# Sliding attention with the values two halves behind the scores, and the first head's scores ahead of its projections

## The chip, the cores and the metric

One core of one Trainium2 chip. The metric is the device time of one execution in microseconds, as a median of the runs. Operands and results are float32; matrix products are made of three products of rounded high parts and low remainders.

## What is computed

The program runs two blocks on 512 tokens of width 1024: a differential attention layer and a sliding-window attention layer with feed-forward parts, then a convolution mixer and a windowed attention with a context of 256 tokens, again with feed-forward parts. The change touches the first two attentions. The first, cut to what matters (8 heads, two score maps of 64 features each per head):

```python
s = jnp.einsum('bqhcd,bkhcd->bhcqk', qblk, k).astype(jnp.float32) * scale
p = jax.nn.softmax(jnp.where(causal, s, NEG_INF), axis=-1)
a = p[:, :, 0] - lam * p[:, :, 1]
return jnp.einsum('bhqk,bkhe->bqhe', a.astype(v.dtype), v)
```

The sliding one (4 key heads, 4 query heads to each, window 128, so a tile of 128 queries sees its own tile of keys and the one before):

```python
s = jnp.einsum('bnqhgd,bnkhd->bnhgqk', qb, kw).astype(jnp.float32) * (1.0 / math.sqrt(HEAD_DIM))
s = jnp.where(valid[None, :, None, None], s, NEG_INF)
m = jnp.maximum(jnp.max(s, axis=-1, keepdims=True), sink)
e = jnp.exp(s - m)
p = e / (jnp.sum(e, axis=-1, keepdims=True) + jnp.exp(sink - m))
o = jnp.einsum('bnhgqk,bnkhd->bnqhgd', p.astype(vw.dtype), vw)
```

## The kernel before

Each engine has an order written out by hand; semaphores join them. Nothing is planned at run time, and each engine takes its instructions in that order. The stages follow each other: `heads` (first attention), its output projection, feed-forward, `kv` and `q` (sliding attention), its output projection, and so on.

**First attention.** A slot is one tile of 128 queries of one head; a head has four slots, and tile i sees i + 1 tiles of keys. TensorE's `slot` (line 2143) makes the scores, transposes the previous slot's weights (`turn`), projects queries, keys and values of one tile of the next head (`project`, line 2082), multiplies the previous slot's values (`values`), and transposes one tile of queries and keys (`turn_qk`). ScalarE's `slot` (983) makes the exponentials (988), copies the transposed weights (960), rounds the weights of the head after next (980), evacuates the projection (940 to 947) and copies turned queries and keys (952). VectorE's `slot` (1678) makes maxima (1683), norm and rotation (`rope`, 1626 to 1632), combines the two maps (1641 to 1646) and makes the low parts of the weights (1673). In the first head the tiles of head 1 were projected one before and one just after the first `turn_qk`, and two in slots 2 and 3.

**Sliding attention.** `swa` runs over 16 groups m of four query heads and one tile (key head m // 4, tile m % 4), each in two halves p = 2m and 2m + 1 of two heads. Names by engine:
- TensorE: `scores(p)` (2303), one masking product of bf16 and four of f32; `turn(p, 0)` (2342) transposes the exponentials; `turn_q(m)` (2295) transposes the queries; `project(m, k0, k1)` (2270) steps k0 to k1 of eight, three matmuls each; `values(p, 0)` (2356); `spread_inverse(m)` (2369); `begun` starts the output projection early.
- ScalarE: `evac_proj(m)` (1087, 1089), `turned(m)` (1095), `exps(p, x)` (1105, x the head in the half), `weights(p, c)` (1117) copies transposed exponentials, `sinks(m)` (1123), `spread_out(m)` (1130) copies the spread inverses out of PSUM, `outs(m)` (1136) the high part of the outputs, `refill` (1148) and `split` (763) high parts of weights.
- VectorE: `maxima(p)` (1836, 1840, 1843), `rotated(m)` (1601 to 1614), `doubled(m)` (1809), `q_low(m)` (1814), `sink_args(m)` (1851), `inverses(m)` (1860, 1862), `outputs(m)` (1867), `low_outs(m)` (1874), `refill` (1311) and `split` (1303) low parts.
- GpSimd: the roots of `rotated` (564) and the widening of the inverses (698).

`outputs(m)` waits for `spread_out(m)`, that for `spread_inverse(m)`, that for the inverses. Scores use three places in PSUM by turns, the transposes two banks by turns in an order that `turn_order` (418) lists: a transpose waits until the one two before it has been read. The context variant of the same function (with 256 context keys) is used by the last attention.

In the loop before, weights of half p are transposed, copied and multiplied in half p + 1, and queries of group m + 2 are turned in the odd half of group m.

Of the kernel before, what the change touches and what calls it, by code (L numbers as in the profile page):

```python
# [178 lines left out]
def program(nc, dram, out):  # L179
    stages = make_plan()  # L180
    stack = ExitStack()
    with stack:
# [25 lines left out]
        half = sbuf("half", [P, 24])  # L208
# [209 lines left out]
        def turn_order(st):  # L418

            order = [("q", 0), ("q", 1)]  # L420
            for p in range(33):
# [286 lines left out]
        def _(act):  # L708
# [222 lines left out]
            def heads(st):  # L931
                S = s_da
# [50 lines left out]
                def slot(h, par, i, first=False, more=True, new=True):  # L983
# [7 lines left out]
                    if not (first and i == 0):  # L991
                        weights(j - 1, (i - 1) % 4)
# [19 lines left out]
                for t in range(3):  # L1012
                    turned(t, t, 0)
# [65 lines left out]
            def swa(st):  # L1079
# [75 lines left out]

                evac_proj(0)
# [5 lines left out]
                for p in range(34):  # L1162
                    m, half = p // 2, p % 2
                    parts = len(chunks(st, p - 1)) if 0 < p < 33 else 0
                    if half == 0 and m < 14:
                        evac_proj(m + 2)
                    if half and m:
                        spread_out(m - 1)
                    if parts:
                        weights(p - 1, 0)  # L1170
                    if p < 32:
                        exps(p, 0)
                    if parts > 1:
                        weights(p - 1, 1)
                    if p < 32:
                        exps(p, 1)
                    if parts > 2:
                        weights(p - 1, 2)
                    if half and m < 16:
                        sinks(m)  # L1180
                    if half and m < 14:
                        turned(m + 2)
                    if half and m:
                        outs(m - 1)
                    if m in (2, 3, 6, 7):
                        refill(m // 4 + 2, p % 4)
                    if p in OUT_SPLITS:
                        split(st["after"], OUT_SPLITS.index(p), OUT_SPLITS.index(p))
# [20 lines left out]
        def _(dve):  # L1209
# [578 lines left out]
            def swa(st):  # L1788
# [112 lines left out]
                for p in range(35):  # L1901
                    m, half = p // 2, p % 2
                    if half == 0 and 0 < m < 17:
                        inverses(m - 1)
                    if half == 0 and m >= 2:
                        low_outs(m - 2)
                    if p < 32:
                        maxima(p)
                    if half and m:
                        outputs(m - 1)  # L1910
                    if half == 0 and 0 < m < 15 and not st["ctx"]:
                        q_low(m + 1)
                    if half == 0 and m < 14:
                        rotated(m + 2)
                        doubled(m + 2)
                    if half and m < 16:
# [28 lines left out]
        def _(pe):  # L1945
# [133 lines left out]
            def heads(st):  # L2079
# [63 lines left out]
                def slot(h, par, i, first=False, more=True):  # L2143
# [11 lines left out]
                    if more and not (first and i < 2):  # L2155
                        project(j + 4, i, 1 - par, h + 1)
# [109 lines left out]
            def swa(st):  # L2266
# [108 lines left out]

                pe.wait_ge(S["kpe"], nt + 1)
# [8 lines left out]
                for p in range(33):  # L2385
                    m, half = p // 2, p % 2
                    parts = len(chunks(st, p - 1)) if p else 0
                    k0 = 4 * half
                    if p < 32:
                        scores(p)  # L2390
                    if parts:
                        turn(p - 1, 0)
# [136 lines left out]
```

## Time and profile before

| | us |
|---|---|
| runs: median (lowest to highest of 3) | 2894.04 (2886.19 to 2899.03) |
| the profiled execution | 2895.21 |
| its span | 2893.2 |
| TensorE busy in it | 2778.1 (96%) |
| VectorE, ScalarE, GpSimd busy | 1777.6, 1115.5, 161.3 |

The profiled execution's own time is the span and 2.0 us around it. The page gives the busy time of each engine, then the span in 40 slices, DMA queues, the chain that ended last, and the costliest groups of instructions. TensorE's busy time counts a modelled end of each matmul, so a start-to-start distance says more about it than a duration. The first head of the first attention lies at 40 to 77 us, the sliding loop at 744 to 905 us.

### The profile page before, as it was taken

The numbers are of one execution on the slowest core, as the hardware profiler recorded it, in microseconds if no ns is written. First come the engines' busy times: TensorE is split into PE (matmuls) and PEld (weight loads), VectorE is DVE, ScalarE is ACT, GpSimd is POOL, SyncE is SP. The second block draws the span as 40 slices with busy tenths as digits, with TensorE's granted clock in tenths as the row PEclk, the third lists the DMA queues.
The fourth block names the chain that finished last, engine by engine and source line by source line (L and its number), as shares of the span: only waits on it lengthen the run. The fifth ranks groups of instructions, "written<-read, shape, count | busy, mean of one in ns | idle before, by whom it ended". The sixth has DMA issues, their size and how long they took to land.

```text
span 2893.2 us, 41339 instructions
## 1 busy us (share of the span) xinstructions
PE 2778.1 (96%) x14371; PEld 2314.3 (80%) x14371; DVE 1777.6 (61%) x2765; ACT 1115.5 (39%) x1869; POOL 161.3 (6%) x205
## 2 busy tenths in 40 slices
PE   7999999999788999999998999999999999999998
PEld 6887788888777778887886888888888887788886
DVE  6775667675765676767885654453456655564645
ACT  5554322224664322223433332231224666442432
POOL 4121000001110000000210000000000000000000
PEclk8999999999999999999998999999999999999999
DMA  3211345452011344542651112112111000222221
GB/s 130 65 45 59 124 164 185 167 182 81 30 37 52 141 172 167 182 148 71 147 139 44 51 59 70 62 58 67 60 57 45 16 30 30 69 99 92 98 89 65
DMA packets 75218, 263.72 MB, mean 91 GB/s; under 512 B 8496, under 2 KB 10800, under 8 KB 73264
## 3 DMA queue, kind: packets, MB, share of 16 engines
q1 hardware_dynamic: 70880, 249.99, 25.1%
q0 software_dynamic: 4176, 11.63, 2.2%
q8 instruction: 94, 1.54, 0.2%
q14 instruction: 68, 0.56, 0.1%
HBM read 247.87 MB, written 2.10 MB: 86 GB/s over the span
## 4 chain that ended last, share of the span: by engine, by line
PE 62%; issue 15%; DVE 13%; ACT 6%; DVEq 2%; ACTq 1%; DMA 1%; POOLq 1%; POOL 0%; SPq 0%
PE psum L1948 16%; PE psum L1950 16%; PE psum L1949 16%; DVE w_lo L1303 2%; PE psum L2113 2%; DVE work L1473 2%; ACT work L1105 2%; PE psum L2091 1%; PE psum L2092 1%; PE psum L2093 1%; PE psum L2365 1%; ACT w_hi L763 1%; ACT sw_pt L1117 1%; DVE work L1591 1%; ACT work L814 1%
## 5 line engine op out<-in xcount | busy, mean ns | idle before, releaser
L1948 PE MATMUL psum<-hx_hi,w_hi 128*128 128x512 f32 x1568 | 622.9, 397 | 4.7 <-DVE hc_lo L1582 1.7
L1950 PE MATMUL psum<-hx_hi,w_lo 128*128 128x512 f32 x1568 | 620.6, 396 | 0.0
L1949 PE MATMUL psum<-hx_lo,w_hi 128*128 128x512 f32 x1568 | 620.0, 395 | 0.0
L763 ACT ACTIVATE w_hi<-w_raw 128x1024 fp32r<-128x1024 f32 (+1 forms) x328 | 344.8, 1051 | 512.8 <-PE psum L1950 207.5
L1303 DVE TENSOR_TENSOR w_lo<-w_raw,w_hi 128x1024 fp32r<-128x1024 f32 (+1 forms) x328 | 398.2, 1214 | 201.1 <-ACT w_hi L763 183.5
L1950 PEld LDWEIGHTS psum<-hx_hi,w_lo 128*128 128x128 f32 x1568 | 295.0, 188 | 70.0
L1948 PEld LDWEIGHTS psum<-hx_hi,w_hi 128*128 128x128 f32 x1568 | 295.0, 188 | 63.7 <-issue 5.4
L1949 PEld LDWEIGHTS psum<-hx_lo,w_hi 128*128 128x128 f32 x1568 | 295.1, 188 | 47.5
L1948 PE MATMUL psum<-a_hi,w_hi 128*128 128x512 f32 (+1 forms) x656 | 233.3, 356 | 9.9 <-DVE a_lo L1413 8.9
L1949 PE MATMUL psum<-a_lo,w_hi 128*128 128x512 f32 (+1 forms) x656 | 232.8, 355 | 0.0
L1950 PE MATMUL psum<-a_hi,w_lo 128*128 128x512 f32 (+1 forms) x656 | 232.6, 355 | 0.0
L1948 PE MATMUL psum<-o_hi,w_hi 128*128 128x512 f32 x544 | 219.7, 404 | 2.7 <-DVE w_lo L1303 2.7
L1949 PE MATMUL psum<-o_lo,w_hi 128*128 128x512 f32 x544 | 217.2, 399 | 0.0
L1950 PE MATMUL psum<-o_hi,w_lo 128*128 128x512 f32 x544 | 217.1, 399 | 0.0
L1435 DVE SCALAR_TENSOR_TENSOR work<-psum,vec,work 128x511 f32<-128x511 f32 (+1 forms) x132 | 83.2, 658 | 162.7 <-ACT work L844 154.4
L564 POOL TENSOR_TENSOR tok_r<-tok_ms,half 128x4 f32<-128x4 f32 (+1 forms) x62 | 67.2, 1084 | 1891.0 <-DVE tok_ms L1231 1577.0
L1377 DVE SCALAR_TENSOR_TENSOR X<-psum,mods,X 128x512 f32<-128x512 f32 x96 | 60.6, 659 | 172.1 <-PE psum L1950 169.8
L844 ACT ACTIVATE work<-psum,vec 128x768 f32<-128x768 f32 (+1 forms) x88 | 70.1, 796 | 220.8 <-PE psum L1950 212.3
L1948 PEld LDWEIGHTS psum<-a_hi,w_hi 128*128 128x128 f32 x656 | 124.3, 190 | 29.4 <-DVE a_lo L1413 9.5
L1948 PE MATMUL psum<-hc_hi,w_hi 128*128 128x256 f32 x512 | 144.6, 282 | 0.0
L1949 PE MATMUL psum<-hc_lo,w_hi 128*128 128x256 f32 x512 | 143.9, 281 | 0.0
L1950 PE MATMUL psum<-hc_hi,w_lo 128*128 128x256 f32 x512 | 143.3, 280 | 0.0
(310 smaller groups left out, 4918.5 us busy)
## 6 DMA issues: line engine op xcount, KB each, us to landing
mod_w<-in_w_mod SPq DMA_DIRECT2D x96, 512.0 KB, 3.7
w_raw<-in_fup SPq DMA_DIRECT2D x88, 512.0 KB, 4.6
w_raw<-in_cup SPq DMA_DIRECT2D x88, 512.0 KB, 3.6
w_raw<-in_fdown SPq DMA_DIRECT2D x32, 512.0 KB, 4.6
w_raw<-in_cdown SPq DMA_DIRECT2D x32, 512.0 KB, 3.6
sw_vb<-tap_prod POOLq DMA_DIRECT2D x29, 391.5 KB, 5.1
w_raw<-in_da_qkv SPq DMA_DIRECT2D x18, 512.0 KB, 3.6
w_raw<-in_fdown SPq DMA_DIRECT2D x16, 384.0 KB, 3.3
```

The lines of the kernel that those rows point to most:

```text
L564: pool.tensor_tensor(tok_r[:, a:b], tok_ms[:, a:b], half[:, a:b], ALU.pow).then_inc(done, 1)
L763: r = act.activation(w_hi[:, off:off + n], w_raw[:, raw:raw + n], ACT.Copy)
L844: act.activation(wk[:, s, 0:toks], ps_of(st, s, 0, toks), ACT.Copy, scale=vec[:, bass.ds(b + col, 1)]).then_inc(s_ctap, 1)
L1105: r = act.activation(work[:, e:e + (w1 - w0)], psum[:, w0:w1], ACT.Exp, bias=neg_max[:, col:col + 1], scale=root, accum_out=row_sum[:, col ...
L1303: r = dve.tensor_tensor(w_lo[:, off:off + n], w_raw[:, raw:raw + n], w_hi[:, off:off + n].bitcast(F32), ALU.subtract)
L1377: r = dve.scalar_tensor_tensor(X[:, b, a:e], ps_of(st, s, a, e), mods[:, l, c, bass.ds(b + o, 1)], X[:, b, a:e], ALU.mult, ALU.add)
L1435: dve.scalar_tensor_tensor(dst[:, a + 1:e], src(a, e - 1), prev, dst[:, a + 1:e], ALU.mult, ALU.add)
L1473: dve.scalar_tensor_tensor(acc, u[:, j:j + n], w, acc, ALU.mult, ALU.add)
L1948: pe.matmul(dst, wh, xh, start=first, stop=False)
L1949: pe.matmul(dst, wh, xl, start=False, stop=False)
L1950: return pe.matmul(dst, wl, xh, start=False, stop=last)
L2113: r = pe.matmul(pb[:, 2 + c, 0:n], qT[rows_, i * P:(i + 1) * P], qT[rows_, SEQ:SEQ + n], start=True, stop=False)
```

## The change

In the first head, `project` for tiles 1 to 3 of head 1 moves to slots 0 to 2, behind the scores, and the second and third `turn_qk` with ScalarE's copies move into slot 0 behind them.

In the sliding attention (not in the variant with context, which keeps its order in functions of its own) the orders of all three engines are new. On TensorE weights of half p are transposed at the end of half p + 1 and multiplied in half p + 2; queries of group m + 1 are turned in the even half of group m, right behind the scores; four projection steps stand in the even half, two and two in the odd; `spread_inverse(m - 1)` moves to the odd half. ScalarE copies the weights of half p - 2 first, and copies turned queries and spread inverses in the even half behind the exponentials. VectorE takes the maxima first in each half, makes the outputs in the even half and low queries, rotation and doubling in the odd one. The loops are one half longer on TensorE and VectorE, two on ScalarE.

```diff
         def turn_order(st):
 
             order = [("q", 0), ("q", 1)]
+            if not st["ctx"]:
+                for p in range(33):
+                    if p % 2 == 0 and 1 <= p // 2 <= 14:
+                        order.append(("q", p // 2 + 1))
+                    if p:
+                        order.append(("e", chunk0(st, p - 1)))
+                return order
             for p in range(33):
...
@@ -988,7 +995,10 @@
                         act.activation(work[:, 1024 * (i % 2) + 512 * c:1024 * (i % 2) + 512 * c + (i + 1) * P],
                                        pb[:, 2 + c, 0:(i + 1) * P], ACT.Exp, bias=neg_max[:, u:u + 1],
                                        accum_out=row_sum[:, u:u + 1]).then_inc(S["ex"], 1)
-                    if not (first and i == 0):
+                    if first and i == 0:
+                        turned(1, 1, 0)
+                        turned(2, 2, 0)
+                    else:
                         weights(j - 1, (i - 1) % 4)
                     if i == 1 and not first:
...
-                for t in range(3):
-                    turned(t, t, 0)
+                turned(0, 0, 0)
                 for i in range(4):
                     slot(0, 0, i, first=True)
...
+                def loop_late(st):
+                    for p in range(36):
+                        m, half = p // 2, p % 2
+                        if 2 <= p < 34:
+                            weights(p - 2, 0)
+                        if half == 0 and m < 14:
+                            evac_proj(m + 2)
+                        if p < 32:
+                            exps(p, 0)
+                            exps(p, 1)
+                        if half == 0 and 1 <= m <= 14:
+                            turned(m + 1)
+                        if half == 0 and m >= 2:
+                            spread_out(m - 2)
+                        if half and m < 16:
+                            sinks(m)
+                        if half and m >= 2:
+                            outs(m - 2)
+                        if m in (2, 3, 6, 7):
+                            refill(m // 4 + 2, p % 4)
+                        if p in OUT_SPLITS:
+                            split(st["after"], OUT_SPLITS.index(p), OUT_SPLITS.index(p))
+
...
-                for p in range(35):
+                for p in range(35 if st["ctx"] else 36):
                     m, half = p // 2, p % 2
-                    if half == 0 and 0 < m < 17:
-                        inverses(m - 1)
-                    if half == 0 and m >= 2:
-                        low_outs(m - 2)
-                    if p < 32:
-                        maxima(p)
-                    if half and m:
-                        outputs(m - 1)
-                    if half == 0 and 0 < m < 15 and not st["ctx"]:
-                        q_low(m + 1)
-                    if half == 0 and m < 14:
-                        rotated(m + 2)
-                        doubled(m + 2)
-                    if half and m < 16:
-                        sink_args(m)
-                    if half and m < 14 and st["ctx"]:
-                        q_low(m + 2)
+                    if st["ctx"]:
+                        if half == 0 and 0 < m < 17:
+                            inverses(m - 1)
+                        if half == 0 and m >= 2:
+                            low_outs(m - 2)
+                        if p < 32:
+                            maxima(p)
+                        if half and m:
+                            outputs(m - 1)
+                        if half == 0 and m < 14:
+                            rotated(m + 2)
+                            doubled(m + 2)
+                        if half and m < 16:
+                            sink_args(m)
+                        if half and m < 14:
+                            q_low(m + 2)
+                    else:
+                        if p < 32:
+                            maxima(p)
+                        if half == 0 and 0 < m < 17:
+                            inverses(m - 1)
+                        if half == 0 and m >= 2:
+                            outputs(m - 2)
+                        if half and m < 16:
+                            sink_args(m)
+                        if half and 1 <= m <= 14:
+                            q_low(m + 1)
+                        if half and m < 14:
+                            rotated(m + 2)
+                            doubled(m + 2)
+                        if half and m >= 2:
+                            low_outs(m - 2)
...
@@ -2152,7 +2205,12 @@
                     if i == 3 and not first:
                         pe.wait_ge(S["qte"], j + 3 if more else 32)
                         turn_outputs(h - 1)
-                    if more and not (first and i < 2):
+                    if first and i < 3:
+                        project(i + 5, i + 1, 1, 1)
+                    if first and i == 0:
+                        turn_qk(1, 1)
+                        turn_qk(2, 2)
+                    if more and not first:
                         project(j + 4, i, 1 - par, h + 1)
                     if not (first and i == 0):
                         if i == 1 and not first:
@@ -2186,10 +2244,6 @@
                 project(4, 0, 1, 1)
                 pe.wait_ge(s_in, 16 * LOADS_IN)
                 turn_qk(0, 0)
-                pe.wait_ge(S["pje"], 2)
-                project(5, 1, 1, 1)
-                turn_qk(1, 1)
-                turn_qk(2, 2)
                 pe.wait_ge(S["pje"], 4)
                 pe.wait_ge(s_constb, 1)
                 for i in range(4):
...
+                def early_output(p):
+                    if p == 27:
+                        pe.wait_ge(S["pje"], 16)
+                    begun(st["after"], 0, (0, 1, 2, 4, 5)[p - 27], (1, 2, 4, 5, 6)[p - 27])
+
+                def loop_late():
+                    for p in range(34):
+                        m, half = p // 2, p % 2
+                        if p < 32:
+                            scores(p)
+                        if half == 0 and 1 <= m <= 14:
+                            turn_q(m + 1)
+                        if half and m < 13:
+                            project(m + 3, 4, 6)
+                        if p >= 2:
+                            values(p - 2, 0)
+                        if half == 0 and m < 13:
+                            project(m + 3, 0, 4)
+                        if half and m < 13:
+                            project(m + 3, 6, 8)
+                        if 27 <= p < 32:
+                            early_output(p)
+                        if 0 < p < 33:
+                            turn(p - 1, 0)
+                        if p == 32:
+                            pe.wait_ge(S["ex"], 30)
+                            begun(st["after"], 3, 0, 6)
+                        if half and m:
+                            spread_inverse(m - 1)
```

`loop_ctx` on each engine is the old loop, called where there is a context; `loop_late` takes its place where there is none. VectorE's loop body is the old one under the condition of a context.

## Rows read from the trace of the kernel before

**Rows 1.** Windows: from:to, length, busy us (xinstructions) by engine; TensorE clock, DMA share, GB/s.

```profile
...
76.00:109.00 33.00, 33.00 (x189) 28.37 (x189) 24.48 (x55) 19.68 (x56) 6.95 (x7) 1.00 0.22 65
745.60:898.80 153.20, 121.92 (x776) 108.35 (x776) 102.77 (x277) 100.54 (x258) 20.32 (x29) 0.92 0.09 32
830.00:832.00 2.00, 2.00 (x8) 1.64 (x7) 1.65 (x5) 0.88 (x4) 1.01 (x1) 0.50 0.02 4
...
```

**Rows 2.** Timeline, first head: start us, us, engine, line, operation, count, [idle before <-releaser].

```profile
...
40.60 0.39 ACT L952 ACTIVATE da_T<-psum 128x256 f32<-128x256 f32 x1 [2.32 <-PE psum L2101]
...
49.89 0.48 PE L2101 MATMUL psum<-ident,da_qk 128*128 128x128 f32 x1 [2.74 <-DVE da_qk L1632]
...
76.91 0.42 PE L2091 MATMUL psum<-w_hi,hx_hi 128*128 128x384 f32 x1
...
```

**Rows 3.** Timeline, same columns: slot 3 of the first head, slot 1 of head 1.

```profile
...
67.60 1.12 PE L2113 MATMUL psum<-da_T 64*128 64x512 f32 x2
...
74.65 1.23 DVE L1673 TENSOR_TENSOR w_lo<-w_raw,w_hi 128x1024 fp32r<-128x1024 f32 x1
...
82.43 0.70 PE L2113 MATMUL psum<-da_T 64*128 64x256 f32 x2
...
83.95 0.42 PE L2091 MATMUL psum<-w_hi,hx_hi 128*128 128x384 f32 x1
```

**Rows 4.** Chain of waits, one sliding group: start us, us, engine, tile written, line.

```profile
...
842.77 0.69 DVE neg_max L1836
...
843.97 0.56 ACT work L1105
...
844.69 0.56 ACT work L1105
...
845.72 0.60 ACT sw_qa L1095
...
846.39 0.43 ACT o_hi L1136
846.85 0.43 DVE o_lo L1874
...
847.36 0.69 DVE neg_max L1836
...
848.62 0.69 DVE sw_qb L1814
...
851.29 0.69 DVE sw_dup L1809
...
852.07 0.69 DVE neg_max L1836
...
```

**Rows 5.** Timeline, columns as in rows 2: sliding steps that the chain lacks.

```profile
...
840.98 0.39 ACT L1130 ACTIVATE sw_invb<-psum 128x256 f32<-128x256 f32 x1 [0.34 <-PE psum L2372]
...
824.73 0.16 DVE L1851 TENSOR_TENSOR sink_e<-neg_max,neg_sink 128x4 f32<-128x4 f32 x1
824.99 0.88 DVE L1311 SCALAR_TENSOR_TENSOR w_lo<-w_raw,vec,w_hi 128x256 fp32r<-128x256 f32 x2
...
```

**Rows 6.** Timeline, TensorE, in the sliding loop.

```profile
...
829.02 0.39 PE L2281 MATMUL psum<-w_hi,hx_hi 128*128 128x256 f32 x1 [1.95 <-ACT sw_sq L1089]
...
```

**Rows 7.** Timeline, start and end of the sliding loop.

```profile
...
748.96 0.42 DVE L1836 TENSOR_REDUCE neg_max<-psum 128x2 f32<-128x256 f32 x1
...
767.45 0.69 DVE L1836 TENSOR_REDUCE neg_max<-psum 128x2 f32<-128x512 f32 x1
...
896.38 0.69 DVE L1836 TENSOR_REDUCE neg_max<-psum 128x2 f32<-128x512 f32 x1
...
904.14 0.69 PE L2353 MATMUL psum<-ident,work 128*128 128x128 f32 x4 [1.55 <-ACT work L1105]
...
```

**Rows 8.** Page, costliest groups: line, operation, count | busy us, mean ns | idle before, releaser.

```profile
...
L763 ACT ACTIVATE w_hi<-w_raw 128x1024 fp32r<-128x1024 f32 (+1 forms) x328 | 344.8, 1051 | 512.8 <-PE psum L1950 207.5
L1303 DVE TENSOR_TENSOR w_lo<-w_raw,w_hi 128x1024 fp32r<-128x1024 f32 (+1 forms) x328 | 398.2, 1214 | 201.1 <-ACT w_hi L763 183.5
...
```

More of the change, by code:

```diff
@@ L1161, in swa @@
                 turned(1)
-                for p in range(34):
-                    m, half = p // 2, p % 2
-                    parts = len(chunks(st, p - 1)) if 0 < p < 33 else 0
-                    if half == 0 and m < 14:
-                        evac_proj(m + 2)
-                    if half and m:
-                        spread_out(m - 1)
-                    if parts:
-                        weights(p - 1, 0)
-                    if p < 32:
[L1172 to L1178, printed above, removed]
-                    if half and m < 16:
[L1180 to L1188, printed above, removed]
+                if st["ctx"]:
+                    loop_ctx(st)
+                else:
+                    loop_late(st)
             for st in stages:
@@ new lines, in loop_ctx @@
+                def loop_ctx():
+                    for p in range(33):
+                        m, half = p // 2, p % 2
+                        parts = len(chunks(st, p - 1)) if p else 0
+                        k0 = 4 * half
+                        if p < 32:
+                            scores(p)
+                        if parts:
+                            turn(p - 1, 0)
+                        if parts > 1:
+                            turn(p - 1, 1)
+                        if half and m < 14:
+                            turn_q(m + 2)
+                        if m < 13:
+                            project(m + 3, k0, k0 + 2)
+                        elif 27 <= p < 32:
+                            early_output(p)
+                        elif p == 32:
+                            pe.wait_ge(S["ex"], 64)
+                            begun(st["after"], 3, 0, 6)
+                        if parts:
+                            values(p - 1, 0)
+                        if parts > 2:
+                            turn(p - 1, 2)
+                        if m < 13:
+                            project(m + 3, k0 + 2, k0 + 4)
+                        for c in range(1, parts):
+                            values(p - 1, c)
+                        if half == 0 and m:
+                            spread_inverse(m - 1)
@@ L2384, in swa @@
                 turn_q(1)
[L2385 to L2392, printed above, removed]
[L2393 to L2416 removed]
+                if st["ctx"]:
+                    loop_ctx()
+                else:
+                    loop_late()
                 wo = st["after"]
```

58 lines of the change are left out of this document (30 added, 28 removed).

## The prediction

> **What bounds the kernel now.** I read the page first (TensorE busy 96% of the span), then the windows, to find the stretches where that is not so, then the timeline and the chain of waits inside them. In head 1 of the first attention TensorE is busy for all 33 us of a 33 us stretch at full clock, so in that stage time saved ahead of it stays saved. In the sliding loop it is busy 121.9 of 153.2 us at a mean clock of 0.92, VectorE 102.8, ScalarE 100.5 [rows 1]: none of the three is full. The reader should look there for what passes the work around.
>
> The chain of waits of one full-width group of two halves shows it [rows 4]. VectorE takes the maxima (842.77), ScalarE does two exponentials (843.97, 844.69), the sinks, the copy of the turned queries (845.72) and the high half of the outputs (846.39), VectorE the low half (846.85), the next maxima (847.36), the queries' low half (848.62), rotation and doubling (851.29), and is back at maxima at 852.07: 9.30 us. TensorE is not in it. Where it does enter, it is through a late evacuation of the projection: a gap of 1.95 us, and TensorE is at 0.50 of its clock right after [rows 1, 6].
>
> In the first head TensorE has nothing to project in its first two slots: one wait alone is 2.74 us (49.89), and head 1's first projection begins at 76.91 [rows 2].
>
> **The change part by part.**
>
> *First head.* The three projections for head 1 move from before slot 0 and slots 2, 3 to slots 0, 1, 2. No instruction is added. The anchor is ScalarE's copy of the first turned queries, which ends at 40.60 + 0.39 = 40.99 [rows 2]; the scores now start there. Costs of the pieces: scores of two tiles plus a turn 83.95 - 82.43 = 1.52; three tiles 0.42 more (1.12 - 0.70 over one head is 0.42 for two tiles more, so 0.21 per tile and head), one tile 0.42 less. Projection, eight value products and two transposes run from 76.91 to 82.43, 5.52; without most of the value products I estimate a projection at 4.3 [rows 2, 3].
> - Slot 0: 41.0 + 1.1 + 4.3 = 46.4, then three pairs of transposes with a ScalarE copy (0.39) between each, about 2.3: 48.7.
> - Slot 1: 1.5 + 4.3 + 0.5 = 6.3: 55.0. Slot 2: 1.9 + 0.1 + 4.3 + 0.7 = 7.0: 62.0.
> - Slot 3 has no projection left, so it is bound by ScalarE and VectorE. In the trace VectorE's low weights for head 2 end 74.65 + 1.23 - 67.60 = 8.28 after the scores of slot 3 begin [rows 3], and head 1's first projection waits for them: 62.0 + 8.3 = 70.3, against 76.91. That is 6.5 us sooner.
>
> What is next late: in slot 3 TensorE now idles about 3 us in three pieces. If the clock falls there, the projection behind it starts at half rate and gives some 1.5 us back, for good, because TensorE is full from then on. Bounds -6.5 and -2 us; I take **-5.5**.
>
> *Sliding attention, the new wait.* Values trail by two halves, and the output steps move. On VectorE an even half is now maxima, inverses, **outputs**; but outputs need the spread inverses, which ScalarE copies only after both exponentials and the turned queries of that same half, and those need these maxima. Before, that copy came first in a half on ScalarE. VectorE is in order, so queued behind the waiting outputs are the odd half's maxima, sink arguments, low queries, rotation and doubling; TensorE's next turn of the queries waits for the doubling, ScalarE's exponentials for the maxima. The new ring, each step by its row:
> - even half: maxima to exponentials 1.20 (843.97 - 842.77), two exponentials 2 x 0.72, turned queries 0.67 (846.39 - 845.72), spread copy 0.39 + 0.05, outputs 0.51 (as 846.85 to 847.36, the same 256 columns): 4.26 [rows 4, 5];
> - odd half: maxima 1.25 (848.62 - 847.36), sink arguments 0.26 (824.99 - 824.73), low queries and rotation 2.67, doubling 0.78, low outputs 0.51: 5.47 [rows 4, 5].
>
> Sum 9.73 against 9.30: the ring gets **longer** by 0.43 us a group. It swaps the sinks (845.72 - 844.69 - 0.72 = 0.31) and the high outputs (0.46) for the spread copy, outputs and sink arguments (0.44 + 0.51 + 0.26). A group whose tile is the first has half the columns; its two reductions are 0.42 rather than 0.69, so 9.19 [rows 4, 7].
>
> *Sliding attention, the waits removed.* TensorE no longer turns the exponentials, has them copied and multiplies them within one half. In steady groups that hides nothing, since TensorE was not in the ring. It pays at the start and around refills. Start: the first maxima at 748.96 do not move. Then two narrow maxima (0.98 each), sink arguments, rotation and doubling (2.67 less the low queries' 0.69 + 0.1, and 0.78: 2.66) give the second group's maxima at 753.8; TensorE's 29 matmuls between doubling and the second half's scores, at the loop's mean of 121.92/776 = 0.157 us, take 4.6 us, to 758.3; 4.96 more (1.25 + 0.26 + 2.67 + 0.78) puts the third group's maxima at 763.3, where the trace has 767.45: 4.1 us sooner [rows 1, 4, 7].
>
> From there to group 14: nine full and three narrow groups, 9 x 9.73 + 3 x 9.19 = 115.1. Eight refill steps on VectorE, 0.88 + 0.1 each, 7.8 [rows 5]; ScalarE's part of them is now beside other work. Two splits of the output weights sit in even halves: ScalarE's 1.05 starts only after the spread copy (3.75), VectorE's 1.21 after that, so the half ends at 6.21 rather than 4.26, twice 1.95 [rows 8]. Group 14: 126.8 after 763.3, that is 890.1. It has no rotation but one split: 9.73 - 2.66 + 1.95 = 9.02, so the last group's maxima are at 899.1 (before 896.38). Its even half has a split and no turned queries: 1.20 + 1.44 + 0.44 + 1.15 + 1.31 = 5.54, to 904.7, and the exponentials end 1.20 + 1.44 later at 907.3 [rows 4, 7].
>
> *The tail.* In the last halves TensorE must multiply half 30 before it turns half 31, but ScalarE copies half 30's weights only after half 31's exponentials, sinks (0.31) and high outputs (0.46), and the copy takes 0.7 (as the turned queries, 512 columns): 908.8; four products at 0.157 make it 909.4. Before, the last turn was at 904.14 [rows 7]. Behind it TensorE has the same full run of output-projection work in both. Loop: 909.4 - 904.14, **+5.3 us**. Ends: -1, if the copies before the turns run further ahead than counted, and +12, by the first rival below.
>
> The sum is -5.5 + 5.3, about 0. The profiled execution took 2895.21 us (span 2893.2), 1.2 above the median of the runs, 2894.04; by it the changed kernel profiles at 2895, and in the median I say **2894.5**.
>
> **The rivals.**
>
> *TensorE becomes late in the odd half.* Between the doubling and the odd half's scores stand 29 matmuls. At 0.157 each that is 4.6 us from 0.6 before the even maxima: ready at 4.0, needed at 4.26. At half clock (8 matmuls in the 2 us from 830, 0.25 each) they take up to 7.2, ready at 6.6, at most 2.3 us late; I take 1.5, since such a stretch need not cover all of them [rows 1, 6]. It decides from the point where the gap ahead of the turned queries reaches about 1.9 us, as the one that went before the 0.50 stretch. For it: VectorE's queue holds TensorE back in every group. Against: the turn of the even half's weights now waits for a bank that the low queries free, which cuts the idle time into about 0.7 and 1.1 us. If half of the 14 groups fall to half clock, + 7 x 1.5 = 10 us (2905); if nearly all, + 20 (2915). The Trainium skill, "TensorE: Matmul & The Clock Gate", section on HAM oscillation, warns only of idle gaps longer than any in this loop; by it this rival would be worth nothing, while the row at 830 shows 0.50 behind a 1.95 us gap, and I go by the row. Chance **0.14**, and this is the slower side.
>
> *The decoupling works as it says.* If the spread copy finds ScalarE free ahead of the exponentials, so that outputs do not wait, VectorE's own work is the ring: 9.73 less the wait of 3.75 - 1.75 = 2.0, near 7.8 us a group, 24 us over the loop less what TensorE then holds back (its 121.9 busy us leave room for it): 2868 to 2880. For it: every TensorE wait of the loop does get another half of time. Against: the order on ScalarE is written out, and the exponentials stand ahead of that copy. Chance **0.08**.
>
> *The first head gives nothing.* Slot 3's waits drop the clock and the low weights for head 2 come no earlier against TensorE: gain 1 us rather than 5.5, 2899. Against: the idle time of slots 0 and 1 is plain in the trace and is filled. Chance **0.14**.
>
> The forecast has **0.64**, with a range of its own from 2887 to 2902.
>
> **How the numbers follow.** The range takes in the first-head rival and the milder half of the late-TensorE one, and below it a loop that costs nothing (-5.3) plus the spread of the runs shown (2886 to 2899): 2883 to 2906. Half a per cent is 14.5 us, about what can be told from no change. Faster by more needs the decoupling rival: 0.08. Slower by more than 2908.5 needs TensorE late in most groups: 0.08. The same: 0.84.
>
> **What would show it.** In the chain of waits of the loop, the ring from one even half's maxima to the next should be 9.6 to 9.9 us, with the outputs idle about 2 us before them, released by the spread copy on ScalarE. The third group's maxima should come near 763 less the first head's gain, all later times shifted alike; the last turn of weights some 5 us later than before relative to the first maxima. Head 1's first projection should start near 70 to 71. The forecast is wrong if outputs do not wait, if a wait of maxima on TensorE's scores is in most groups, or if the clock over the loop is under 0.88.

## The result, and the profile after

The changed kernel takes 2903.65 us (median of 17 runs, 2898.89 to 2911.3) against 2894.51 us for the kernel before (17 runs beside them): ratio 1.0027, 95% interval 1.002 to 1.0034. That is 9.1 us slower, within half a per cent. It is inside the range of 2883 to 2906, 2.35 us under its upper end, and just outside the range of 2887 to 2902 that the forecast itself had. The profiled execution of the changed kernel took 2906.14 us. Its page begins so (busy us, share, xinstructions):

```profile
span 2904.1 us, 41339 instructions
...
PE 2781.3 (96%) x14371; PEld 2316.1 (80%) x14371; DVE 1777.9 (61%) x2765; ACT 1114.7 (38%) x1869; POOL 160.3 (6%) x205
```

TensorE is as full as before by its share; the loss has to be looked for in the stages where it is not.

The sliding loop does what the chain was summed up to do. Chain of waits of one group (start us, us, engine, tile written, line), the answer to [rows 4]:

```profile
845.24 0.69 DVE neg_max L1874
...
847.90 0.60 ACT sw_qa L1104
...
848.63 0.39 ACT sw_invb L1139
849.05 0.42 DVE sw_osb L1905
...
849.56 0.69 DVE neg_max L1874
...
853.74 0.69 DVE sw_dup L1847
...
854.53 0.42 DVE o_lo L1912
...
855.04 0.69 DVE neg_max L1874
```

From maxima to maxima it is 9.80 us, where it was 9.30. The spread copy (`sw_invb`) stands behind the exponentials and the turned queries, and VectorE's outputs (`sw_osb`) behind it. What engines waited for in 735 to 910 us (waiting line <- releaser: us in total, times, longest us):

```profile
DVE sw_osb L1905 <- ACT sw_invb L1139: 26.8, 14, 2.0
...
PE psum L2419 <- ACT sw_pt L1126: 22.2, 14, 3.0
...
PE psum L2353 <- DVE sw_dup L1847: 16.1, 15, 1.5
...
DVE neg_max L1874 <- PE psum L2392: 4.0, 2, 2.3
```

VectorE waits for the copy fourteen times, once a group, up to 2.0 us each, and the odd half's work is queued behind these waits. The maxima wait for TensorE only twice, so TensorE does not set the groups. Windows of the changed kernel (columns as in [rows 1]): 33 us from head 1's first projection; the sliding loop from first to last group's maxima; and the end of that loop.

```profile
71.78:104.78 33.00, 33.00 (x184) 28.55 (x183) 24.22 (x55) 19.57 (x55) 6.94 (x7) 0.98 0.22 65
746.77:900.13 153.36, 113.10 (x731) 100.30 (x730) 97.38 (x262) 96.39 (x249) 19.66 (x28) 0.94 0.09 32
...
892.00:899.00 7.00, 5.53 (x16) 4.48 (x17) 3.52 (x7) 3.22 (x9) 0.00 (x0) 0.53 0.23 75
```

The clock over the loop is 0.94 (before 0.92), so it is not half rate that makes the loop long, except at its end. Timeline of the changed kernel there and in the first head (columns as in [rows 2]):

```profile
67.31 1.65 PE L2186 MATMUL psum<-da_v,da_aT 128*128 128x128 f32 x6 [1.64 <-ACT da_aT L967]
...
71.78 0.67 PE L2144 MATMUL psum<-w_hi,hx_hi 128*128 128x384 f32 x1
...
887.72 0.69 DVE L1874 TENSOR_REDUCE neg_max<-psum 128x2 f32<-128x512 f32 x1
...
893.47 2.07 PE L2419 MATMUL psum<-sw_pt,sw_vb 128*128 128x256 f32 x4 [2.96 <-ACT sw_pt L1126]
...
900.13 0.69 DVE L1874 TENSOR_REDUCE neg_max<-psum 128x2 f32<-128x512 f32 x1 [2.27 <-PE psum L2392]
```

Head 1's first projection starts at 71.78 instead of 76.91 [rows 2], 5.1 us sooner, but it takes 0.67 us instead of 0.42, at half rate behind slot 3's waits.

Stage by stage, in us. The stages are cut at the first operation of each norm (VectorE's reading of `tok_ms` from PSUM). Each entry is the mean, the lowest and highest, and the number of the profiled executions with the order named; for the sliding stage these are the versions with the order of before or of the change, without the variants further down:

```
stage                      old order             new order             difference
heads (first attention)    289.7 (287.4-290.6) 5   287.6 (283.8-288.6) 9   -2.1
sliding attention          239.7 (237.5-241.8) 5   249.0 (246.7-250.8) 4   +9.3
network behind the convolution     567.2 or 574.0          567.2 or 574.0           see below
first profile of each kernel: heads -3.0, sliding +7.4, network behind the convolution +6.8,
all else -0.3; sum +10.9, the 10.9 us between the two profiled executions
```

### The profile page after: what moved, and what is told of

The parts are those of the page before. It is cut to its first block, busy times and chain, and to the rows that moved or that the text cites. A ratio compares the mean times of both kernels' runs of the same rounds, so it can differ in the third digit from the quotient of the medians.

```text
span 2904.1 us, 41339 instructions
## 1 busy us (share of the span) xinstructions
PE 2781.3 (96%) x14371; PEld 2316.1 (80%) x14371; DVE 1777.9 (61%) x2765; ACT 1114.7 (38%) x1869; POOL 160.3 (6%) x205
## 4 chain that ended last, share of the span: by engine, by line
PE 64%; issue 15%; DVE 12%; ACT 6%; DVEq 2%; POOLq 1%; ACTq 0%; POOL 0%
PE psum L2001 17%; PE psum L2002 17%; PE psum L2003 17%; DVE w_lo L1341 2%; PE psum L2166 2%; ACT work L1114 2%; DVE work L1511 1%; PE psum L2144 1%; PE psum L2145 1%; PE psum L2146 1%; PE psum L2419 1%; ACT w_hi L770 1%; ACT sw_pt L1126 1%; DVE work L1629 1%; ACT work L821 1%
```

## Experiments: the two parts apart

The theory is that the first head gains and that the sliding order loses by the wait it puts on VectorE. The rival is something else in either part.

**head_only.** The kernel before with the first head's new order; what is projected and turned there, and nothing else of the diff.

```diff
+                    if first and i < 3:
+                        project(i + 5, i + 1, 1, 1)
...
-                for t in range(3):
-                    turned(t, t, 0)
+                turned(0, 0, 0)
```

> The changed order of the first head alone, in the kernel before; the sliding attention keeps its old order. Theory one (the first head gains what the trace of after shows, 4 to 5 us, and a clock drop at that stage's end takes part of it back): ratio to before 0.998 to 0.9995, head 1's first projection near 71 us rather than 76.9. Rival (the convolution feed-forward loops, 8.37 us a block before and 8.48 after, run slower because of how the new program is laid out): if that hangs on the first head's new order, the blocks here take 8.48 and the ratio is 1.000 to 1.001. Second rival (the block's length is drawn anew in each execution): it can be either here, whatever the order.

Measured: 2895.51 us, ratio 0.9997 (0.9988 to 1.0006). Its heads stage is 287.5 us, 3.1 under the 290.6 of the first profile of before, and 2.2 under the mean of the old order; the median can't be told from no change. Its network behind the convolution took 574.0 us, which the text had as the rival's sign; that is taken up further down.

**slide_only.** The changed kernel with the old first head.

> The new order of the sliding attention alone; the first head as before. Theory one (VectorE waits about 2 us in every group for the copy of the spread inverses, and the last halves wait for half 30's weights): slower by 6 to 8 us, ratio 1.002 to 1.003, ring of 9.8 us, fourteen waits of outputs on that copy of 1.7 to 2.0 us each. Rival (TensorE and its clock are what is late): the wait of the maxima on TensorE's scores is over 8 us in sum. Third (most of the measured 9 us lies in unchanged loops): ratio under 1.0015.

Measured: 2906.04 us beside 2896.0, ratio 1.0033 (1.002 to 1.0046). Heads 290.5, sliding 249.8. The fourteen waits of up to 2.0 us are there (26.9 us in all), and the maxima wait for TensorE once, 3.2 us, where the rival had over 8. The 10.0 us are over the 6 to 8 expected; the interval, 5.8 to 13.3 us, takes them in. The two parts, -0.5 and +10.0, add up to 9.5 where the whole change measured 9.1: no sign that they interact.

## Experiments: the wait on VectorE

**spread_first.** The changed kernel; in an even half ScalarE does the spread copy first.

```diff
                         if 2 <= p < 34:
+                            if half == 0 and m >= 2:
+                                spread_out(m - 2)
                             weights(p - 2, 0)
...
-                        if half == 0 and m >= 2:
-                            spread_out(m - 2)
```

> The changed kernel with one step moved: in each even half ScalarE copies the spread inverses first, ahead of the weights and the exponentials, not behind the turned queries. Theory one (that place is the cause of the slower ring): VectorE's 2 us wait ahead of the outputs goes; the ring falls from 9.8 us towards VectorE's own 7.8, but the products of TensorE (7.3 us a group plus waits for banks) may hold it at 8.2 to 9; over 14 groups 11 to 22 us less than the changed kernel, so 2882 to 2893, ratio to before 0.996 to 0.9995. Rival (TensorE's late scores bound the ring): it stays above 9.5 us, the wait of outputs turns into one of maxima on the scores, and the time stays within 3 us of the changed kernel's 2903.

Measured: 2886.51 us, ratio 0.9966 (0.9951 to 0.9981) to before; the sliding stage 232.7 instead of 248.9 us, 16.2 less, and the full-width groups without refill or split take 7.85 to 9.04 us. Timeline, VectorE in an even half:

```profile
833.81 0.69 DVE L1874 TENSOR_REDUCE neg_max<-psum 128x2 f32<-128x512 f32 x1
...
835.67 0.42 DVE L1905 TENSOR_TENSOR sw_osb<-psum,sw_invb 128x256 f32<-128x256 f32 x1
837.37 0.69 DVE L1874 TENSOR_REDUCE neg_max<-psum 128x2 f32<-128x512 f32 x1 [1.28 <-PE psum L2392]
...
842.85 0.69 DVE L1874 TENSOR_REDUCE neg_max<-psum 128x2 f32<-128x512 f32 x1
```

The outputs start without a wait, and the next wait is 1.28 us for TensorE's scores. This group takes 9.04 us (842.85 - 833.81) where the changed kernel took 9.80: part of the 2.0 us comes back as a wait for TensorE. TensorE's clock rises too, from a mean of 0.94 over the loop to 0.99, and how much of the 16.2 us is by that was not taken apart. Moving one copy turned a loss of 9 us into a gain of 9.5.

**outputs_late.** The same wait taken away from the other side: ScalarE as in the changed kernel, VectorE's outputs moved from the even to the odd half, behind its maxima.

> The changed kernel with VectorE's step outputs moved from the even half (behind the inverses) to the odd half (behind its maxima), so that ScalarE keeps its order, spread_out behind the exponentials and the turned queries. Theory (the new wait of 2.0 us on VectorE sets the length of a group, because the odd half's maxima are queued behind it): the wait vanishes as well as with spread_out moved first, the group goes from 9.8 to 8.3 to 8.8 us, the sliding stage from 248.9 to 233 us (231 to 236) and the time to 2888 us (2884 to 2892). Rival (what helped there was ScalarE's order itself, the weights or exponentials coming at another place): no gain, 2903 to 2907 us, and a group of 9.8 us.

Measured: 2895.18 us, ratio 0.9995 (0.9983 to 1.0007); the sliding stage 239.65 us. Of the 16.2 us of spread_first 9.2 come back, so neither text was right. Timeline, VectorE:

```profile
841.59 0.69 DVE L1874 TENSOR_REDUCE neg_max<-psum 128x2 f32<-128x512 f32 x1 [1.80 <-PE psum L2392]
...
842.84 0.42 DVE L1905 TENSOR_TENSOR sw_osb<-psum,sw_invb 128x256 f32<-128x256 f32 x1
...
847.58 0.69 DVE L1874 TENSOR_REDUCE neg_max<-psum 128x2 f32<-128x512 f32 x1
```

The wait for the copy is gone in this group (three are left in the loop and behind it, 5.2 us in all, one of 4.2 that spread_first has too). But the step's own time now lies in the odd half, where VectorE has no gap: 847.58 - 841.59 = 5.99 us, where spread_first has 842.85 - 837.37 = 5.48. In the even half the step was covered by the wait for scores, which is 1.80 here and 1.28 there. Group by group the loss against spread_first is 0.5 us in six groups, 0 to 0.4 in six, and 0.9 to 1.0 in the three from the first split of the output weights on (from the maxima at 847.58 in this version); 7.0 in all, the missing part. The step's own 0.51 us explains about half of the last three; what else is in them was not tested. VectorE's waits for ScalarE's high halves at the splits grew from 7.9 to 12.0 us, and TensorE's clock in these three groups was 0.96, 0.89 and 0.80 where spread_first had 1.00. So a wait can be removed from either engine, and the two are not worth the same: it counts in which half the step then stands.

**before_spread_last.** The wait put into the old order: the kernel before, with the spread copy of the odd half behind both exponentials.

```diff
-                    if half and m:
+                    if half and m and st["ctx"]:
                         spread_out(m - 1)
...
                     if p < 32:
                         exps(p, 1)
+                    if half and m and not st["ctx"]:
+                        spread_out(m - 1)
```

> The kernel before with one step moved: in the sliding stage's odd half ScalarE does spread_out behind both exponentials instead of first. The same wait is so put into the old order. Spread_out then starts at about 845.4 instead of 841.0, VectorE's outputs waits about 1.8 us in a place where it had none, the high outputs follow at 847.5 instead of 846.4, the low outputs and the next half's maxima at 848.5 instead of 847.36. Theory (the position of spread_out on ScalarE alone can cost this): a group goes from 9.30 to about 10.4 us, 14 groups give +15 us, time 2911 us (2905 to 2917). Rival (in the old order the wait lies beside VectorE's other idle time and is absorbed): a group stays at 9.3 to 9.5 us, 2895 to 2898 us.

Measured: 2913.55 us, ratio 1.0059 (1.0042 to 1.0076); the sliding stage 258.5 us; steady groups of 10.48 us. Timeline, the odd half of such a group, then the row of the kernel before that the second one answers to:

```profile
867.16 0.42 DVE L1869 TENSOR_TENSOR sw_osb<-psum,sw_invb 128x256 f32<-128x256 f32 x1 [1.97 <-ACT sw_invb L1130]
...
868.21 0.16 DVE L1862 TENSOR_TENSOR sw_sum<-row_sum,sink_e 128x4 f32<-128x4 f32 x1 [0.37 <-ACT sink_e L1123]
```

```profile
845.77 0.16 DVE L1860 TENSOR_TENSOR sw_sum<-row_sum,sink_e 128x4 f32<-128x4 f32 x1 [1.06 <-ACT sink_e L1123]
```

A wait of 1.97 us costs 1.18 us a group (10.48 - 9.30). Most of the rest covers idle time that VectorE had anyway: of its wait of 1.06 us for the sinks 0.37 is left. The expected group (10.4 us) and time (2911 us, 2905 to 2917) came as worked out. For the place of this one copy the chain gave both signs and the sizes to a few us; for the other move, outputs_late, it did not.

## Experiments: the tail and the splits

**spread_first_tail.** spread_first, and in half 32 TensorE turns half 31 and does its output work ahead of the values of half 30.

> As spread_first, and at the end of the loop TensorE turns half 31 and starts the output projection of the fourth block before it multiplies half 30's values. Theory (TensorE idles there for ScalarE's copy of half 30's weights, which stands behind half 31's exponentials): 1.5 to 2.5 us less than spread_first. Rival (the idle time is only moved to the next wait, the weights of half 31): the same as spread_first within 0.5 us.

Measured: the sliding stage 231.0 us, 1.7 less than spread_first; the time 2888.11 us, ratio 0.9966 (0.9953 to 0.9978), the same as spread_first. From the last group's maxima to the end of the stage it is 55.0 us instead of 57.1, but the next version, which keeps the old order there, has 55.6. One profile of each, of a stage that differs by 4 us between profiles of one kernel, does not show the gain; it stays open.

**spread_first_lo_late.** spread_first, with VectorE's low halves of the output weights split one half later.

```diff
-                    if p in OUT_SPLITS:
-                        split(st["after"], OUT_SPLITS.index(p), OUT_SPLITS.index(p))
+                    if p - 1 in OUT_SPLITS and not st["ctx"] or p in OUT_SPLITS and st["ctx"]:
+                        q = p if st["ctx"] else p - 1
+                        split(st["after"], OUT_SPLITS.index(q), OUT_SPLITS.index(q))
```

> The changed kernel with ScalarE's spread_out first in the even half, and besides, in the sliding stage, VectorE's low half of each output weight block split (four of 1.22 us) one half later, after the odd half's work. There VectorE waited 7.9 us in four places (up to 2.2 us) for ScalarE's high half. Theory (VectorE's queue is on the ring, so each of these waits lengthens a group): the waits go, the sliding stage falls from 232.7 to about 227 us (225 to 230), the time to 2881 us (2877 to 2885). Rival (TensorE or ScalarE sets these groups already): 232 to 233 us, 2885 to 2889 us.

Measured: the sliding stage 227.4 us, 5.3 less than spread_first and as worked out; the time 2884.26 us, ratio 0.9953 (0.9937 to 0.9969), the lowest median here, though its interval overlaps that of spread_first. The 5.3 us lie where the splits are: 3.8 in three groups and 1.5 behind the last maxima. Waits in the sliding loop: spread_first, then the row of spread_first_lo_late that comes nearest; in the latter the waits of `w_lo` inside the loop are gone (one of 0.5 us is left, behind it).

```profile
DVE neg_max L1874 <- PE psum L2392: 8.7, 9, 1.8
DVE w_lo L1341 <- ACT w_hi L770: 7.9, 4, 2.2
```

```profile
DVE neg_max L1874 <- PE psum L2393: 10.6, 12, 1.8
```

VectorE's wait for TensorE's scores is the one that grows, from 8.7 to 10.6 us. That suggests that TensorE would be the next to set the groups; no run tests it.

## Experiments: what differed without being changed

The first profile of the changed kernel had 6.8 us more in the network behind the convolution, in which no instruction differs. Windows inside that stage: the kernel before, first profile; the same kernel in its third. Same length, TensorE busy throughout at a granted clock of 1.00:

```profile
1700.00:1800.00 100.00, 100.00 (x574) 87.69 (x573) 47.58 (x63) 28.65 (x30) 0.00 (x0) 1.00 0.20 68
1800.00:1900.00 100.00, 100.00 (x576) 87.77 (x575) 42.05 (x57) 24.66 (x26) 0.00 (x0) 1.00 0.18 59
```

```profile
1700.00:1800.00 100.00, 100.00 (x567) 87.13 (x566) 44.75 (x61) 25.84 (x27) 0.00 (x0) 1.00 0.20 65
1800.00:1900.00 100.00, 100.00 (x569) 87.13 (x568) 42.75 (x58) 25.67 (x27) 0.00 (x0) 1.00 0.18 58
```

Some 575 matmuls in 100 us or some 568. Five more profiles of versions already measured were taken to tell a property of the version from one of the execution.

> The kernel before, unchanged, for a second profiled execution. Open is why the feed-forward network behind the convolution took 567.2 us in the first profile of the kernel before and 574.0 us in the five profiles taken of other versions, although no instruction of that stage differs. Theory: it is a state of the single execution, not of the version; its blocks of 48 matmuls go at either 8.37 or 8.48 us. Then this second profile can show 574 us there too (five of six did), and the span is then 2900 us rather than 2893; whatever it shows, the stages of the sliding layer and the heads keep their 241.5 and 290.6 us to 0.5 us. Rival: the kernel before has 567 us there each time, because something that it leaves behind (a place of code or of a buffer) differs from the others; then 567 again.

> The changed kernel, unchanged, for a second profiled execution. By the theory that the rate of the blocks is drawn anew in each execution, the stage behind the convolution takes 567 or 574 us, and the mix before it 281.9 or 285 us; by the rival it is 574 us again and the mix 281.9. Either way the sliding stage takes 248.9 us and the heads 287.6 us, each within 0.5 us, so that the change itself costs about 7.4 - 3.0 = 4.4 us plus 0 to 1 us around it.

Measured: before 567.2 us again, the changed kernel 574.0 again. That, with before_spread_last at 567.2 and all other versions at 574.0, spoke for the version.

> The kernel before, unchanged, a third profiled execution. In the network behind the convolution the matmuls of the 512 and 256 column mix go at one of two rates, 14.4 or 16.7 ns a matmul above their columns' time at 2.4 GHz. Two profiles of the kernel before and the one with its spread_out moved, whose TensorE program is the same, showed 14.4 (567.2 us for the stage); the six others with a changed TensorE program and the second of the changed kernel showed 16.7 (574.0 us). Theory A (the rate there goes with the version): 14.4 and 567.2 us again, span 2889 to 2894 us. Theory B (drawn in each execution, seen 3 to 7 so far by chance): 16.7 and 574.0 us in about two of three, span then 2896 to 2900 us.

> The changed kernel, unchanged, a third profiled execution. Theory A (the rate goes with the version): 574.0 us in the network behind the convolution for the third time, span 2897 to 2905 us. Theory B (drawn in each execution): 567.2 us there in about one of three, span then 2891 to 2898 us. The sliding stage takes 248.9 and the heads 287 us by both, as its order is not in question.

> The kernel before with the new order of the first head alone, a second profiled execution. Theory A (the rate behind the convolution goes with the version): 574.0 us there again; its heads' stage keeps the 3.0 us gain (287.5 us against 290.6), so that the version gains in the heads what it pays behind the convolution. Theory B: 567.2 us in about one of three, and the span then falls to about 2889 us.

Measured: the kernel before showed 574.0 in its third profile; the changed kernel and head_only 574.0 again. So one and the same version can have either, and the rate is not a fixed property of the code. Over all 14 profiled executions it was 567.2 three times and 574.0 eleven times. All three lie among the four profiles in which TensorE's program is that of before. If the version had no influence, that would happen in 4 of 364 ways to place the three, about 1 in 90. This suggests that the version shifts the odds, and does not show it. It bears on the result: the two stages that the change touches account for -2.1 + 9.3 = 7.2 us of the 9.1 in the medians, and a shift of these odds could be the rest. This stays open, and so does the cause.

The repeated profiles show the second source of scatter. The sliding stage of the kernel before took 241.5, 237.5 and 237.5 us, its heads 290.6, 289.4 and 287.4; in the changed kernel these were 248.9, 246.7 and 250.8, and 287.6, 283.8 and 288.4. Two of the texts had both stages repeating within 0.5 us, and the third profile's text had 248.9 and 287; that was wrong. Timeline of TensorE at the same instruction, first and third profile:

```profile
829.02 0.39 PE L2281 MATMUL psum<-w_hi,hx_hi 128*128 128x256 f32 x1 [1.95 <-ACT sw_sq L1089]
...
830.07 1.91 PE L2365 MATMUL psum<-sw_pt,sw_va 128*128 128x256 f32 x4
```

```profile
824.22 0.38 PE L2281 MATMUL psum<-w_hi,hx_hi 128*128 128x256 f32 x1 [1.95 <-ACT sw_sq L1089]
...
825.04 1.05 PE L2365 MATMUL psum<-sw_pt,sw_va 128*128 128x256 f32 x4
```

The gap is the same 1.95 us; behind it the four value products take 1.91 us once and 1.05 us the other time. Over the loop of the kernel before the mean clock was 0.92 in the first profile and 0.95 in the other two.

## Why the prediction was right, and where not

**The ring (right).** Predicted 9.73 us for a full group, 9.6 to 9.9 in the chain, with outputs idle about 2 us behind the spread copy; measured 9.80, and 14 waits of up to 2.0. Between the third group's maxima and group 14's the text has 126.8 us; the trace of the changed kernel has 887.72 - 759.93 = 127.8, refills and splits included.

**The start (right in sign, a little small).** The third group's maxima come 13.2 us after the first (759.93 - 746.77), predicted 14.3, before 18.5 in the first profile and 17.4 and 17.5 in the other two. In slide_only it is 14.7.

**The last two groups (mis-sized).** Predicted 9.02 us from group 14's maxima to the last group's; measured 12.41 (900.13 - 887.72), 10.24 in the second profile and 12.61 in the third. Two terms were missing. The low outputs of that group have no rotation before them any more and wait 1.19 us for ScalarE's high outputs, which the sum counted as 0.51 without a wait; this is the 1.2 us of the second profile, here on its timeline:

```profile
892.01 0.43 DVE L1912 TENSOR_TENSOR o_lo<-sw_osb,o_hi 128x256 fp32r<-128x256 f32 x1 [1.19 <-ACT o_hi L1145]
892.54 0.69 DVE L1874 TENSOR_REDUCE neg_max<-psum 128x2 f32<-128x512 f32 x1
```

And TensorE's wait for weights behind the split is 2.96 us; in the first and third profile the clock is at 0.53 and 0.56 behind it, and the maxima then wait 2.27 and 2.46 us for scores. In the second profile the wait of 2.96 us is the same and the clock stays at 1.00. That is the first rival in one group instead of seven, 2.2 us rather than 10. Elsewhere it cost the ring nothing: the gap before the turned queries is 1.05 us in steady groups, as argued, and two groups in which the clock was 0.88 and 0.83 took 9.81 us.

**The tail (right in the mean).** From the last group's maxima to the end of the stage 57.1 us against 55.7 in the first profiles; means over three profiles of each 57.6 and 54.7, 2.9 for the 2.5 us predicted.

**The base (not seen).** The stage was compared with a profile of before that took 241.5 us, 4 us more than two later ones, with a mean clock of 0.92 instead of 0.95 over the loop. Against that same profile the stage lost 7.4 us where 5.3 was predicted; against the mean of old-order profiles it lost 9.3. Rows at 0.50 of the clock stood in [rows 1] and the text took them as part of the kernel; a second execution would have shown them to be partly a draw.

**The first head (the step that failed).** Predicted -5.5, bounds -6.5 and -2. The gain arrives as worked out: 5.1 us at head 1's first projection, 5.7 counted from the stage's start (71.78 - 30.51, before 76.91 - 29.96), and 5.0 still at the last head's values (259.72 - 30.51, before 264.18 - 29.96). At the stage's end 3.0 are left in the first profiles and 2.1 in the mean. The text said that TensorE is full from then on and gave back 1.5 us once, behind slot 3; up to the last head's values it was 0.7. It overlooked that the stage ends with gaps as well, and 2.0 us are lost there. There the changed kernel shows a gap of 2.05 us and the kernel before one of 1.72, and the matmuls behind them run at different rates; timeline and window of the changed kernel, then the window of before:

```profile
271.15 1.07 PE L2179 MATMUL psum<-ident,work 128*128 128x128 f32 x4 [2.05 <-DVE work L1684]
```

```profile
271.00:275.67 4.67, 4.52 (x19) 3.95 (x20) 0.09 (x1) 0.60 (x1) 0.00 (x0) 0.63 0.00 0
```

```profile
275.16:280.00 4.84, 4.84 (x27) 4.22 (x28) 0.69 (x1) 1.73 (x9) 0.00 (x0) 1.00 0.00 0
```

The same products behind this gap, up to the next output weights, take 4.28 us in the changed kernel (275.43 - 271.15) and 2.70 before (277.86 - 275.16): 1.6 of the 2.0 us. It goes with the new order: 4.28 us at a clock of 0.60 in eight of its nine profiles, 2.7 at 1.00 in all five of the old order, behind gaps of 2.05 to 2.21 and 1.68 to 1.86 us. The one exception, after_again, had a gap of 1.86 and full clock, and its stage of 283.8 us is the shortest. Between it and before_third, the one profile of the old order with no half rate there either, the gain is 3.6 us.

**Sum.** Predicted -5.5 + 5.3, about 0; measured in the medians of the parts -0.5 and +10.0. Both terms erred to the same side, and the change ended 9 us above the 2894.5 that was said. The measured 0.27% lies in the 0.84 for no change beyond half a per cent, but that owes more to the width of half a per cent (14.5 us) than to the sum: the forecast's own range, with a chance of 0.64, was missed by 1.7 us, and the result fell in the part added for the rivals. The rival that the first head gives nothing had the size (a gain of 1 us, the median's is 0.5) and not the way: the gain was there at head 1, and part of it went at the stage's end. The decoupling rival (2868 to 2880, a ring of 7.8 us) needed the spread copy ahead of the exponentials; spread_first is that version, and it reached 7.85 to 9.04 us in full groups and 2886.5 us, as TensorE's scores and the splits then hold back VectorE.

## What to carry to other kernels

A step moved to give one engine slack is priced by what stands before its input on the other engine and by what is queued behind it on its own. Here a copy of 0.39 us placed behind the exponentials held back a whole half of VectorE's work by 2 us, and its place was worth 16 us in the stage. Sum the chain once round by rows; it gave the group to 0.07 us. Before small differences are read from a stage, profile the same kernel two or three times, and take a gain as kept only up to the next stretch where the engine idles.

## What the runs showed of the hardware

- TensorE's matmuls of 512 and 256 columns with TensorE busy throughout and the granted clock at 1.00 ran at one of two rates: some 575 or some 568 in 100 us, a stage of 567.2 or 574.0 us, in one and the same kernel (before, first and third profile). The rate held through that whole stage; in the stage before it (the mix), whose matmuls have the same two shapes, it changed within a profile: 48 matmuls took 8.37 us and from one place on 8.48 in the changed kernel's first profile, and 8.48, then 8.37 in that of the kernel before. The stages whose matmuls have 512 columns alone did not show it (the second network took 382.7 us in 13 of 14 profiles). The cause is open.
- A gap of 1.95 us at the same instruction was followed by half rate in one execution and by full rate in another (1.91 and 1.05 us for the same four products; before, first and third profile). So was a gap of 2.96 us (2.07 and 1.13 us for four products; the changed kernel, first and second profile). The Trainium skill, "TensorE: Matmul & The Clock Gate", section on HAM oscillation, warns of longer gaps alone; this case shows half rate behind 1.95 us and behind 2.96, though not each time.
